# Even layer of a transformer block: one convolution per attention job, and filter and spectra in one row behind the attention

## The reference

```python
def hyena_filter_freq(L, w1, b1, w2, b2, w3, freq, decay):
    ...
    hid = jnp.sin(fr * (z @ w1.astype(f32) + b1.astype(f32)))
    hid = jnp.sin(fr * (hid @ w2.astype(f32) + b2.astype(f32)))
    h = (hid @ w3.astype(f32)).reshape(L, 2, HY_WIDTH)
    h = h * jnp.exp(-t[:, :, None] * jnp.abs(decay.astype(f32))[None])
    h_pos, h_neg = h[:, 0], h[1:, 1]
    norm = jnp.sqrt(jnp.sum(h_pos * h_pos, axis=0) + jnp.sum(h_neg * h_neg, axis=0))
    h_circ = jnp.concatenate([h_pos, jnp.zeros((1, HY_WIDTH), f32), h_neg[::-1]], axis=0) / norm
    return jnp.fft.rfft(h_circ, axis=0)

def hyena(u, conv_w, conv_b, bias, filt):
    L = u.shape[1]
    x0, x1, v = jnp.split(short_conv(u, conv_w, conv_b), 3, axis=-1)
    z = v * x1
    hf = hyena_filter_freq(L, *filt)
    zf = jnp.fft.rfft(z.astype(jnp.float32), n=2 * L, axis=1)
    y = jnp.fft.irfft(zf * hf[None], n=2 * L, axis=1)[:, :L].astype(z.dtype)
    return x0 * (y + z * bias)

def even_mixer(h_c, h_l, w_in, w_out, ...):
    ...
    q_l = rope_2d(q_l, pos_row, pos_col)
    k_l = rope_2d(k_l, pos_row, pos_col)
    y_l = jnp.concatenate([hyena(p_l[..., :i_q], conv_w, conv_b, hy_bias, filt),
                           latent_window_attention(q_l, k_l, v_l, k_c, v_c, sink)], axis=-1) @ w_out
    ...
```

## Time and profile before

| | |
|---|---|
| runs | 2607.24, 2611.62, 2613.82 us (median 2611.62) |
| profiled execution | 2605.64 us, its span 2603.8 us, mean granted TensorE clock 0.98 |
| TensorE busy | 2497.8 us (96%) |
| VectorE, ScalarE, GpSimd busy | 1629.0, 1190.7, 367.0 us |
| even layer, as TensorE has it | some 1380 to 1680 us from the span's start |

### The profile page before, as it was taken

The page is one execution under the profiler, slowest core; times in us unless marked ns, Lnnn a source line. Parts: engine busy times, 40 slices in busy tenths (PEclk is TensorE's granted clock), DMA queues, the critical chain, the costliest instruction groups (busy, mean ns, idle before and its releaser), DMA issues.

```text
span 2603.8 us, 42299 instructions
## 1 busy us (share of the span) xinstructions
PE 2497.8 (96%) x18041; PEld 2319.9 (89%) x18041; DVE 1629.0 (63%) x2438; ACT 1190.7 (46%) x1950; POOL 367.0 (14%) x385
## 2 busy tenths in 40 slices
PE   8999989999999999999999988999999999999998
PEld 7999978999999898899998655888888999999998
DVE  4787466777887865667774876542443654556753
ACT  5444456544344355555444543431332534344653
POOL 1311000332023000022331220200001011011000
PEclk9999899999999999999999999999999999999999
DMA  7667544567676766347775220233322423334552
GB/s 237 211 220 219 154 135 119 166 223 235 228 233 223 230 154 190 113 126 250 259 262 156 58 68 1 75 104 97 97 98 88 129 90 115 99 108 141 166 195 98
DMA packets 386385, 401.65 MB, mean 154 GB/s; under 512 B 44695, under 2 KB 370611, under 8 KB 385940
## 3 DMA queue, kind: packets, MB, share of 16 engines
q1 hardware_dynamic: 383448, 391.19, 48.1%
q10 hardware_dynamic: 2748, 7.76, 0.8%
HBM read 394.72 MB, written 4.19 MB: 153 GB/s over the span
## 4 chain that ended last, share of the span: by engine, by line
PE 74%; DVE 17%; ACT 5%; issue 2%; DMA 1%; POOL 1%; ACTq 0%; DVEq 0%; SPq 0%
PE bank L672 22%; PE bank L673 21%; PE bank L674 21%; DVE rounded L2332 6%; PE bank L680 3%; DVE plain L2321 3%; ACT rounded L1588 2%; PE bank L685 2%; PE bank L1524 1%; DVE plain L2579 1%; POOL plain L3379 1%; ACT plain L1778 1%; PE bank L1087 1%; PE bank L1117 0%; DVE plain L2456 0%
## 5 line engine op out<-in xcount | busy, mean ns | idle before, releaser
L672 PE MATMUL bank<-rounded 128*128 128x256 f32 (+1 forms) x3704 | 1120.4, 302 | 22.2 <-DVE rounded L2332 17.8
L673 PE MATMUL bank<-rounded 128*128 128x256 f32 (+1 forms) x3704 | 1102.4, 298 | 0.0
L674 PE MATMUL bank<-rounded 128*128 128x256 f32 (+1 forms) x3704 | 1101.7, 297 | 0.0
L2332 DVE TENSOR_TENSOR rounded<-plain,rounded 128x1024 fp32r<-128x1024 f32 (+1 forms) x618 | 722.6, 1216 | 518.9 <-ACT rounded L1588 518.7
L672 PEld LDWEIGHTS bank<-rounded 128*128 128x128 f32 x3704 | 717.5, 194 | 57.2 <-DVE rounded L2332 20.3
L1588 ACT ACTIVATE rounded<-plain 128x1024 fp32r<-128x1024 f32 (+1 forms) x630 | 616.8, 1032 | 327.9 <-PE bank L674 283.7
L673 PEld LDWEIGHTS bank<-rounded 128*128 128x128 f32 x3704 | 717.5, 194 | 16.4
L674 PEld LDWEIGHTS bank<-rounded 128*128 128x128 f32 x3704 | 717.1, 194 | 16.5
L672 PE MATMUL bank<-rounded,rounded 128*128 128x256 f32 (+2 forms) x1472 | 452.6, 307 | 19.9 <-DVE rounded L2332 16.5
L673 PE MATMUL bank<-rounded,rounded 128*128 128x256 f32 (+2 forms) x1472 | 449.9, 306 | 0.0
L674 PE MATMUL bank<-rounded,rounded 128*128 128x256 f32 (+2 forms) x1472 | 448.6, 305 | 0.0
(11 more groups left out here) (306 smaller groups left out, 1988.3 us busy)
## 6 DMA issues: line engine op xcount, KB each, us to landing
plain<-in_mlp_w SPq DMA_DIRECT2D x64, 1024.0 KB, 5.3
plain<-in_ada_w SPq DMA_DIRECT2D x48, 1024.0 KB, 5.4
plain<-in_ffn_w_gate SPq DMA_DIRECT2D x44, 1024.0 KB, 5.8
plain<-in_ffn_w_up SPq DMA_DIRECT2D x44, 1024.0 KB, 5.9
plain<-in_ffn_w_down SPq DMA_DIRECT2D x32, 1024.0 KB, 5.2
plain<-in_w_in SPq DMA_DIRECT2D x32, 1024.0 KB, 5.6
plain<-in_od_w_in SPq DMA_DIRECT2D x32, 1024.0 KB, 5.7
plain<-in_ffn_w_down SPq DMA_DIRECT2D x16, 768.0 KB, 5.1
```

The source lines that it names most:

```text
L672: pe.matmul(dst, a[0], b[0], start=first and i == 0, stop=False)
L673: pe.matmul(dst, a[0], b[1], start=False, stop=False)
L674: ins = pe.matmul(dst, a[1], b[0], start=False, stop=last and i == n - 1)
L2332: dve.tensor_tensor(low, raw, top, SUB).then_inc(*done(("lo", m, half)))
```

## The change

- `BESIDE` has one convolution per job, jobs 0 to 10; the net's two layers follow in jobs 2 and 4; jobs 8 and 10 have ScalarE's DMAs for the taps' weights and decays, and the decays' absolute value.
- VectorE does then(i+1) ahead of the job's convolution, and takes over `lo` for the convolution's units from GpSimd, after the rest of the job.
- Everything else of `taps` stands behind the attention: transposes (the first sequence's ahead of the last third), four taps products, the first sequence's spectra, the response, the second's spectra, the norm, the first way back, the attention half of the first output block, the second way back. z by rows has a place of its own (`zk`) instead of the taps'.
- The norm is 16 products with one column each (`ncol`, 128x4) instead of two of 512 columns; the four squares are summed in PSUM (GpSimd's addition is gone); root and reciprocal work on 128x4. The response is copied by ScalarE without the norm, which is applied behind the way back, together with a bias product that ScalarE does beforehand.
- Each of the first four rotation products comes one product later.
- The first output block's hyena half waits for each remainder by itself, and VectorE does a remainder one step after its gate.

```diff
-BESIDE = ([("conv", i) for i in range(3)] + [("net", 0)] + [("conv", i) for i in (3, 4)] + [("net", 1)]
-          + [("conv", i) for i in range(5, 12)] + [("taps", i) for i in range(14)])
+BESIDE = [("conv", 0)] + [slot for i in range(12) for slot in (
+    ("conv", i + 1) if i < 11 else None, {2: ("net", 0), 4: ("net", 1), 8: ("decays", 0), 10: ("size", 0)}.get(i))]
@@ tensor_program, even
                         lambda: broadcast(was, 0)).then_inc(*done((s, "q", 0), (s, "q", 1), ("unit", m)))
                 here(s, "begun", "pe")
-                turned(0)
...
-                    turned(1 + j)
+                    turned(j)
...
+        turned(2)
         turned(3)
...
+        def power():
+
+            b = bank(s, "rn")
+            for x in new(at(s, "hsq")):
+                pe.wait_ge(*x)
+            for j in range(4):
+                ins = plain(b[:, j:j + 1], [(b_.Hh[:, a, j * 128:j * 128 + 128], M.ones[:, 0:1]) for a in range(4)])
+            ins.then_inc(*done((s, "rn")))
...
             if i + 1 < n:
                 scores(i + 1)
+            else:
+                byrows(0)
             beside(2 * i + 1)
             third(i)
             beside(2 * i + 2)
-        for i in range(2 * n + 1, len(BESIDE)):
-            beside(i)
         here(s, "attended", "pe")
...
+        byrows(1)
+        for tile in range(2):
+            for d in range(2):
+                taps(tile, d)
+        spectrum(0)
+        for kc in range(2):
+            for a in range(2):
+                response(kc, a)
+        spectrum(1)
+        power()
+        back(0)
+        bs0 = [bank(s, "wo", j) for j in range(2)]
+        for k in range(4, 8):
+            for j in range(2):
+                outer(k, j, bs0[j])
+        back(1)
         here(s, "turned", "pe")
@@ scalar_program, even
+        byrows(0)
+        for d in range(2):
+            decayed(1, d)
+        byrows(1)
+        spectrum(0)
...
+        act.activation(b_.Hh, b_.Hh, ACT.Square, bias=0.0, scale=1.0).then_inc(*done((s, "hsq")))
+        for kc in range(2):
+            for a in range(2):
+                for x in new(at(s, "hf", kc, a), at(s, "tapd", 1, 1)):
+                    act.wait_ge(*x)
+                act.activation(b_.Hf[:, a * 2 + kc, :], M.bank(s, "hf", kc, a)[:, :], ACT.Copy, scale=2.0 / 512).then_inc(
+                    *done((s, "hfv"), ("free", s, "hf", kc, a)))
+        for j in range(4):
+            act.activation(b_.z[:, j, :], b_.z[:, j, :], ACT.Copy, scale=col("hy_bias_2", j)).then_inc(*done((s, "zb", j)))
+        spectrum(1)
...
@@ vector_program, even
             if i + 1 < n:
                 first(i + 1)
+                then(i + 1)
+            else:
+                here(s, "attended", "dve")
+                byrows(0)
             beside(2 * i + 1)
-            if i + 1 < n:
-                then(i + 1)
             kept(i)
             beside(2 * i + 2)
...
+            if i + 1 < n and CONV[i + 1][2]:
+                lo(U[(s, "cv", *CONV[i + 1][0:2])] + 3)
+        byrows(1)
+        for tile in range(2):
+            for d in range(2):
+                taps(tile, d)
+            evenodd(tile)
         for q in range(2):
             for kc in range(2):
...
+                filtered(q, kc)
+        for x in new(at(s, "rnroot")):
+            dve.wait_ge(*x)
+        dve.reciprocal(M.ncol, M.ncol).then_inc(*done((s, "rnk")))
         for q in range(2):
...
+            back(q)
@@ gpsimd_program, even
-        for n in range(12):
-            part, blk, jj = CONV[n]
-            if jj:
-                lo(U[s, "cv", part, blk] + 3)
-        for x in new(at(s, "hsqa")):
-            pool.wait_ge(*x)
-        pool.tensor_tensor(b_.Hh[:, 0:2, :], b_.Hh[:, 0:2, :], b_.Hh[:, 2:4, :], ADD).then_inc(*done((s, "hsq")))
```

More of the change, by code:

```diff
@@ new lines, in taps, with response @@
+        def taps(tile, d):
+            b = bank(s, "tap", tile, d)
+            for x in new(at(s, "hy", 1, "s"), at("decay")):
+                pe.wait_ge(*x)
+            pe.matmul(b[:, :], b_.hd[1][0:64, tile * 128:tile * 128 + 128], b_.w3[0:64, d * 512:d * 512 + 512],
+                      start=True, stop=True).then_inc(*done((s, "tap", tile, d)))
+        def response(kc, a):
+            b = bank(s, "hf", kc, a)
+            mat, v = ((b_.cm, b_.P_), (b_.sm, b_.N_))[a]
+            for x in new(at(s, "PN"), at("dft")):
+                pe.wait_ge(*x)
+            plain(b[:, :], [(mat[:, tile, kc * 128:kc * 128 + 128], v[:, tile, :]) for tile in range(2)]).then_inc(
+                *done((s, "hf", kc, a)))
@@ new lines, in decays, with size @@
+        def decays():
+            for x in new(at(s, "cvo", 2, 3), at(s, "qk", 4)):
+                act.wait_ge(*x)
+            act.dma_start(b_.w3[0:64, :], M.t["hy_w3_2"][0]).then_inc(*M.land("phase0").done())
+            act.dma_start(b_.dec_, M.t["hy_decay_2"].rearrange("a d n -> (a d n)").partition_broadcast(128)).then_inc(
+                *M.land("phase0").done(("decay",)))
+        def size():
+            for x in new(at("decay")):
+                act.wait_ge(*x)
+            act.activation(b_.dec, b_.dec, ACT.Abs, bias=0.0, scale=1.0).then_inc(*done((s, "dec")))
@@ new lines, in decayed, with byrows @@
+        def decayed(tile, d):
+            for x in new(at(s, "dec"), at("dft")):
+                act.wait_ge(*x)
+            act.activation(b_.tw[tile][d], b_.dec[:, d, :], ACT.Exp, bias=0.0, scale=b_.ex[:, tile:tile + 1]).then_inc(
+                *done((s, "tw", tile, d)))
+        def byrows(q):
+            for x in new(at(s, "zt", q, 1), at(s, "ao", len(b_.jobs) - 1)):
+                act.wait_ge(*x)
+            act.activation(b_.zk[:, q * 2 + 1, :], M.bank(s, "zt", q, 1)[:, :], ACT.Copy, scale=1.0).then_inc(
+                *done((s, "zk", q, 1), ("free", s, "zt", q, 1)))
@@ L2074, in beside @@
                 hidden(x)
+            elif kind == "decays":
+                decays()
             else:
-                taps(x)
+                size()
         def weights(x):
```

283 lines of the change are left out of this document (118 added, 165 removed).

## The result

Four runs of the changed kernel gave a median of 2579.62 us (2574.21 to 2583.92), beside four of the kernel before with 2610.72 (2607.24 to 2613.82): a ratio of 0.9882, 95% interval 0.9869 to 0.9895, so faster by 31 us, clear of the noise. The prediction was 2583.8 with a range of 2572 to 2601. The profiled execution took 2579.67 us, its span is 2577.9 against 2603.8 before.

The account below looks back on a forecast made before the run. TensorE, busy for 96% of the span, was taken to bound the kernel. Opening -5.3, attention -26.8 and end +4.3 sum to -27.8, from a median of 2611.62 to 2583.8 us, range 2572 to 2601.

Parts of the forecast that it names:

- The opening: Rotations a product later remove TensorE's 3.74 us wait and the slow clock behind it: -5.3 us, bounds 3.74 to 5.4.
- A job without a wait: Attention job with one convolution: 9.2 us of TensorE's own time, next probabilities ready with 1.4 us of slack.
- VectorE's period: VectorE's work for a pair of attention jobs: 16.9 us beside 18.4 of TensorE, so it fits (92%).
- Job 0: First attention job: 9.2 us plus 2.0 for its slow start, 11.2 together.
- The net jobs: Two attention jobs with the filter's small net: 2.7 us wait plus 1.1 low clock each, 7.6 for both.
- The last job: Last attention job, without a convolution: 5.3 us, of which 1.9 is TensorE waiting for ScalarE.
- The end: Last attention product to first output block's second half: 48.3 us, the norm 3.7 of it, filter steps covered; +4.3.
- A: Rival: attention jobs with one convolution stay at 10.1 us, as measured once; -19 in sum, 2592.8 us; chance 0.15.
- D: Rival: nets, splits and low clock bring the attention's period to 11.5 us; no net change, 2609 us; chance 0.08.
- B: Rival: filter steps at the layer's end come one step late in both sequences; +8, 2591.8 us; chance 0.10.
- C: Rival: the weight split on VectorE takes each of eleven attention jobs to 15.09 us; net +27.5, 2639 us; chance 0.04.
- The sum: Whole kernel: opening -5.3, attention -26.8 and end +4.3 give -27.8 us; chance 0.63.

Follow-up runs that it names:

- the second execution: The changed kernel run once more with no edit: 2583.28 us, ratio 0.9892 to the kernel before.

## Why the prediction was right

Point by point, by its own steps:

- **The opening** (-5.3, measured -5.6): shown in both directions, and in full: the clock is 1.00 where the wait stood, so the bound of 5.4 held and not the 3.74 of a clock that falls anyway. What the prediction had at nothing is the second fall of the clock in the first attention job, 1.6 us more that go with the early rotation.
- **A job without a wait** (9.2, measured 8.8): from second to second 8.81 in the last four full jobs. I took the 9.2 from a job in which the second waited between its two halves; a second whose probabilities are both there takes 1.09 and not 1.45. Over ten jobs this is -3.9 us. The step held and its term was mis-sized: "third adds 1.10 less overlap: 9.2".
- **VectorE's period** (16.9 of 18.4 for a pair): it fits in the jobs without the net; a job with a split costs TensorE 0.20 between the halves of one second. In the two jobs with the net the split does count: it stands with 2.3 us ahead of the late maxima, and with the nets in jobs without a split the waits were 1.31 and 0.35.
- **Job 0** (11.2, measured 9.34): -1.9. I carried over the 2.0 us of the slow start before. 1.6 of them were the low clock that the runs show only together with the early rotation; 0.36 between the halves of the second is left.
- **The net jobs** (7.6 for both): everything above 8.81 in jobs 1 to 10 is 8.5. The intervals are 11.2 and 11.1 where I named 13. The waits are 2.31 and 2.20 where I took 2.69 each, the low clock cost 1.6 and came behind the second only (in the second execution behind neither), and I hadn't counted the net's own products (1.1) and seconds whose halves come apart (1.3). The low clock, by stretch:

```profile
1499.30:1501.50 2.20, 2.20 (x10) 1.37 (x10) 2.11 (x4) 0.60 (x1) 0.00 (x0) 0.59 0.00 0
```

  The scores there take 1.71 instead of 1.14 and the convolution 6.74 instead of 5.74.
- **The last job** (5.3 with 1.9 of waiting, measured 5.12 with 2.12): the wait is ScalarE's as forecast. ScalarE's rows ahead of it:

```profile
1543.60 2.00 ACT L1619 ACTIVATE rounded<-plain 128x1024 fp32r<-128x1024 f32 x2
...
1545.76 1.05 ACT L2084 ACTIVATE plain<-plain 128x1024 f32<-128x1024 f32 x1
1546.71 1.08 ACT L1822 ACTIVATE plain<-bank 128x512 f32<-128x512 f32 x2
```

  The split, the copy of the attention's result and the decays' absolute value stand ahead of the probabilities' copy.
- **The end** (+4.3, measured +5.9 in this execution): the norm's sixteen columns cost 3.7, as the distance in the earlier trace rows said, and not nothing as their width says. The filter steps were covered as worked out (19.4, 27.6 and 35.9 us after the attention against 18.9, 27.3 and 35.6). What I hadn't priced is the clock behind the norm, +1.6 here, and +9.9 in the second execution, where it was low behind the last third as well.
- **The rivals.** A (10.1 per job) and D (11.5) fall with the 8.8 (9.7 as the mean of jobs 1 to 10, nets included). B falls: no way back waits. C falls with the split; a loss did come, 7 us, but from late scalings, which the change had taken away.
- **The sum** (-27.8; -31.5 in this execution, -24.7 in the second): the forecast lies between the two. That it comes out so near is in part luck: the attention came out 5.0 us shorter than forecast and the end 1.6 longer, and the clock alone moved the end by 8 us from one execution to the next.

## What to carry to other kernels

Where an in-order engine serves two chains, what the critical engine waits for goes first, and the work that waits for that engine's fresh result goes behind it: one call moved was 37 us of attention here with one convolution per job, and 12 with two. Filler work is best spread over all the jobs that have a latency to hide; packed two to a job it leaves the last jobs bare (13.8 us). And price a narrow f32 product by its weight load: in the norm's rows the weight load is busy without a gap (1.90 of 1.90 us), and sixteen products of one column were 3.7 us, about as long as four of 512 columns (half of the 6.97 for eight). Last, idle time of TensorE costs more than its length: with late scalings 21.7 us of it brought 15.6 us of slower work, with two convolutions per job 8.1 brought 5.7.

## What the runs showed of the hardware

- The granted clock can be low in a stretch in which TensorE has no idle time by its rows: down to 0.50 (1.2 GHz) behind sixteen one-column products, and 0.50 for 10 us behind thirty-two. It is no property of the kernel alone: of two executions of the same kernel one had 0.51 for 14 us behind a 2.12 us wait, the other had 1.00 there.
- It can also differ by what happened long before: behind the same two waits of 1.31 and 0.36 us in the first attention job it fell to between 0.52 and 0.55 in the three executions that had waited 3.7 us in the opening, 40 us earlier, and stayed at 1.00 in the eleven that hadn't. In between it had come back to 1.00.
- One-column products slow down with the clock, 19 matmuls in 2 us at 1.00 and 11 at 0.50.
- While GpSimd does a weight split, 4.7 to 5.2 us, single VectorE operations on other data take 2.34 instead of 0.69 and 1.72 instead of 0.28; most of the operations beside the same GpSimd instruction keep their usual time. So the price depends on which operation falls together with what, and isn't a factor on all.
